# One core: modulation rows brought forward, and index scores computed between the slabs of two projection groups

## The reference, cut to what matters

```python
c_act = silu(c)
mod = c_act @ w_mod + b_mod                   # 6 x 2048: shift1, scale1, gate1, shift2, scale2, gate2
h = rms_norm(x, g_pre_mix) * (1 + scale1) + shift1
q, k, v, q_idx, k_idx, w_idx, pool_in, lru_in, lru_gate = split(h @ w_in)
dots = einsum('qhd,sd->qhs', q_idx, k_idx)    # 16 index heads of 64
score = einsum('qh,qhs->qs', w_idx, relu(dots)) / 32, then top 128 keys per query
logits = q k / sqrt(128) + rel_bias[bucket(distance)]
```

## Time and profile before

| | us |
|---|---|
| median of 3 runs | 2516.28 (2509.43 to 2518.47) |
| the profiled execution, its own time | 2509.14 |
| span of its instructions | 2507.0 |
| PE busy in the span | 2388.7 (95%) |
| DVE / ACT / POOL busy | 1213.4 / 684.5 / 362.5 |

### The profile page before, as it was taken

How to read it: one execution, slowest core, us unless ns; L and a number is a source line. 1 busy time by engine, 2 the same in 40 slices (tenths; PEclk the granted TensorE clock), 3 DMA queues, 4 the chain that set the end, 5 groups by cost and what they waited for, 6 DMA issues and landing times.

```text
span 2507.0 us, 27318 instructions
## 1 busy us (share of the span) xinstructions
PE 2388.7 (95%) x10722; PEld 1880.6 (75%) x10722; DVE 1213.4 (48%) x1586; ACT 684.5 (27%) x896; POOL 362.5 (14%) x247
## 2 busy tenths in 40 slices
PE   4898899999997999899999999999999999999997
PEld 1456687778776788788888888888888888888885
DVE  5536966699329765643333234343243332333336
ACT  2332624222326422422122122121121221221222
POOL 3543054444427200000000000000000000000000
PEclk8999999989999999999999999999999999999998
DMA  4987266733314276522332332323322333323324
GB/s 180 364 338 272 93 235 235 262 128 95 91 61 129 97 268 244 135 84 93 93 93 94 97 94 92 92 84 100 99 93 92 84 100 95 97 93 92 93 93 168
DMA packets 137504, 340.89 MB, mean 136 GB/s; under 512 B 15824, under 2 KB 17488, under 8 KB 123216
## 3 DMA queue, kind: packets, MB, share of 16 engines
q1 hardware_dynamic: 132208, 331.12, 39.6%
q10 hardware_dynamic: 5216, 8.66, 0.9%
HBM read 322.70 MB, written 16.79 MB: 135 GB/s over the span
## 4 chain that ended last, share of the span: by engine, by line
PE 85%; DVE 7%; DMA 3%; ACT 2%; issue 2%; ACTq 1%; POOL 0%; SPq 0%; DVEq 0%; POOLq 0%
PE psum L694 27%; PE psum L696 27%; PE psum L695 27%; DMA mod_slab<-in_w_mod 2%; DVE acc_a L1394 2%; DMA raw<-in_w_in 1%; PE psum L773 1%; PE psum L758 1%; PE psum L742 1%; PE psum L803 1%; ACT sq_out L1044 0%; DVE pt_lo L1712 0%; PE psum L735 0%; DVE probs L1699 0%; ACTq L1063 0%
## 5 line engine op out<-in xcount | busy, mean ns | idle before, releaser
L1755 DVE TENSOR_TENSOR w_lo<-raw,w_hi 128x1024 fp32r<-128x1024 f32 x256 | 311.7, 1224 | 744.1 <-ACT w_hi L1281 743.7
L694 PE MATMUL psum<-h_hi,w_hi 128*128 128x512 f32 (+1 forms) x1616 | 645.9, 400 | 11.5 <-POOL w_lo L634 5.5
L695 PE MATMUL psum<-h_lo,w_hi 128*128 128x512 f32 (+1 forms) x1616 | 644.6, 399 | 0.0
L696 PE MATMUL psum<-h_hi,w_lo 128*128 128x512 f32 (+1 forms) x1616 | 643.9, 398 | 0.0
L1281 ACT ACTIVATE w_hi<-raw 128x1024 fp32r<-128x1024 f32 x256 | 271.2, 1060 | 1014.9 <-PE psum L696 1005.8
L694 PE MATMUL psum<-w_hi,u_hi 128*128 128x512 f32 x1024 | 408.3, 399 | 0.0
L696 PE MATMUL psum<-w_hi,u_lo 128*128 128x512 f32 x1024 | 403.6, 394 | 0.0
L695 PE MATMUL psum<-w_lo,u_hi 128*128 128x512 f32 x1024 | 401.5, 392 | 0.0
L694 PEld LDWEIGHTS psum<-h_hi,w_hi 128*128 128x128 f32 (+1 forms) x1616 | 306.1, 189 | 91.3 <-issue 9.2
L696 PEld LDWEIGHTS psum<-h_hi,w_lo 128*128 128x128 f32 (+1 forms) x1616 | 306.1, 189 | 75.7 <-issue 0.2
L695 PEld LDWEIGHTS psum<-h_lo,w_hi 128*128 128x128 f32 (+1 forms) x1616 | 306.0, 189 | 74.3 <-issue 0.2
(11 more groups left out here) (256 smaller groups left out, 2064.1 us busy)
## 6 DMA issues: line engine op xcount, KB each, us to landing
raw<-in_w_mlp_up SPq DMA_DIRECT2D x128, 512.0 KB, 3.7
raw<-in_w_mlp_down SPq DMA_DIRECT2D x128, 512.0 KB, 3.7
mod_slab<-in_w_mod SPq DMA_DIRECT2D x48, 1024.0 KB, 5.9
raw<-in_w_in SPq DMA_DIRECT2D x88, 512.0 KB, 5.9
mod_ring<-in_w_mod_first SPq DMA_DIRECT2D x32, 1024.0 KB, 9.0
raw<-in_w_out SPq DMA_DIRECT2D x32, 512.0 KB, 5.8
slab<-in_w_mod SPq DMA_DIRECT2D x16, 1024.0 KB, 4.9
bias_s<-bias_out ACTq DMA_DIRECT2D x32, 256.0 KB, 6.1
```

Source lines behind the costliest of these rows:

```text
L694: nc.tensor.matmul(o, a_hi, b_hi, start=first, stop=False)
L695: nc.tensor.matmul(o, a_hi, b_lo, start=False, stop=False)
L696: return nc.tensor.matmul(o, a_lo, b_hi, start=False, stop=last)
L1755: V.tensor_tensor(w_lo[:, local % RING, :, :], raw[:, local % RING, :, :], w_hi[:, local % RING, :, :].bitcast(F32), ALU.subtract).then_in ...
```

## The change

At the start: the bias table and its shifted copy come inside the packed columns, so that ACT's eight DMAs are gone. The sums of squares use 32 columns of the ones matrix for each of four tiles side by side, in one bank; ACT copies that bank to `x_rows`, and one matmul with a selecting matrix `pick` adds the four rows and spreads them over all partitions. ACT squares a quarter of x at a time and stores one bias bank after each. `x_norm` follows the steps of the eighth bank, scales nothing, and two tiles of x are scaled in each block; `softplus` follows the third block. The memsets on POOL are put in another order, those of `stat` and `inv_n` after the table.

In the middle: the `dots` stages are gone. After each slab of g2 and g3 PE does the dots of two pairs (three after slabs 24 and 25, none after slab 31), in banks 4 to 7 in turn; the turn of the index weights follows slab 16. In ACT's loop the slab 19 + j is rounded and then the ReLUs of the pairs after slab 16 + j are taken. In DVE's loop the modulation slabs of slab 16 + j are added and then the dots of those pairs. The modulation slabs go three to two weight slabs up to slab 31, then one each up to slab 55. The two copies of the index key are issued by ACT, before it takes the high part of s1, and no longer by SP.

```diff
 MOD_EARLY = 2 * KD
 MOD_BLOCKS = KD // KS
 MOD_PROJ = 3 * KD
-MOD_DOTS = 3 * SG
-MOD_AGAIN = 3 * SG + 3
+MOD_AGAIN = 4 * SG
+MOD_MORE = 3 * SG
 def mods_beside(s):
-    if 2 * SG <= s < 3 * SG:
+    if 2 * SG <= s < 4 * SG:
         i = s - 2 * SG
         first = MOD_EARLY + 3 * (i // 2) + 2 * (i % 2)
         return [first] if i % 2 else [first, first + 1]
-    if MOD_AGAIN <= s < MOD_AGAIN + 2 * KD:
-        return [MOD_EARLY + KD + s - MOD_AGAIN]
+    if MOD_AGAIN <= s < MOD_AGAIN + MOD_MORE:
+        return [MOD_EARLY + MOD_MORE + s - MOD_AGAIN]
     return []
...
 STAGES = (
-    [("s0", "AD"), ("s1", "AD"), ("g2", "AD"), ("widx", "D")]
...
+DOT_PAIRS = TT * IH // 2
+PAIRS_AFTER = (2,) * SG + (3, 3) + (2,) * (SG - 3) + (0,)
+assert sum(PAIRS_AFTER) == DOT_PAIRS and sum(PAIRS_AFTER[:SG]) == DOT_PAIRS // 2
+DOT_BANK = 4
 def dots_of(n):
-    pair, n = divmod(n, 2 * IH)
-    return 2 * pair + n % 2, n // 2
+    return n % TT, n // TT
+def pairs_after(i):
+    return range(sum(PAIRS_AFTER[:i]), sum(PAIRS_AFTER[:i + 1]))
...
                 for g in mods_beside(s):
                     load_mod(g)
                 load_slab(s + 2)
-                if s == 2 * SG + 2:
-                    sp.wait_ge(idx_ready, 1)
-                    sp.dma_start(ki_hi[1][ID:P, :].bitcast(F32), ki_hi[0][0:ID, :].bitcast(F32)).then_inc(key_copied, 16)
-                    sp.dma_start(ki_lo[1][ID:P, :].bitcast(F32), ki_lo[0][0:ID, :].bitcast(F32)).then_inc(key_copied, 16)
-                if s == MOD_DOTS:
-                    for t in range(TT):
-                        load_mod(DOTS_MOD + t)
                 if s == MOD_AGAIN + 1:
                     sp.wait_ge(score_done, 1)
...
+            ch.link(nc.gpsimd.memset(pick[:], 0.0))
+            for q in range(4):
+                ch.put(nc.gpsimd.memset(pick[32 * q:32 * q + 1, :], 1.0))
             ch.wait()
             pool.sem_inc(consts, 1)
...
-            for k in range(KD):
-                pe.wait_ge(xsq_ready, k + 1)
-                last = nc.tensor.matmul(psum[:, XSUM_BANK, :], ones[:], x_sq[:, k, :], start=k == 0, stop=k == KD - 1)
+            pe.wait_ge(blk_ready, 1)
+            for q in range(TT):
+                bias_bank(q)
+                pe.wait_ge(xsq_ready, 4 * q + 4)
+                for j in range(4):
+                    last = nc.tensor.matmul(psum[32 * j:32 * j + 32, XSUM_BANK, :], ones[:, 0:32], x_sq[:, 4 * q + j, :],
+                                            start=q == 0, stop=q == TT - 1)
             last.then_inc(xsum_done, 1)
-            pe.wait_ge(blk_ready, 1)
-            for i in range(BIAS_FIRST):
+            pe.wait_ge(consts, 1)
+            pe.wait_ge(xrows_ready, 1)
+            nc.tensor.matmul(psum[:, XALL_BANK, :], pick[:], x_rows[:], start=True, stop=True).then_inc(xall_done, 1)
+            for i in range(TT, BIAS_FIRST):
                 bias_bank(i)
...
-            group(G_QI + 1, STAGE["g2"], features_out, h)
-            n = STAGE["widx"]
-            begin(n)
-            pe.wait_ge(widx_copied, 1)
-            for t in range(TT):
-                last = nc.tensor.transpose(bank(n, 0)[:, IH * t:IH * t + IH], widx_t[ID:KW, P * t:P * t + P],
-                                           ident[ID:KW, ID:KW])
-            last.then_inc(stage_done, 1)
-            pe.wait_ge(key_copied, 32)
-            for m in range(TT * IH // 4):
-                if m == 0:
+            def key_weights():
+                n = STAGE["widx"]
+                begin(n)
+                pe.wait_ge(widx_copied, 1)
+                for t in range(TT):
+                    last = nc.tensor.transpose(bank(n, 2)[:, IH * t:IH * t + IH], widx_t[ID:KW, P * t:P * t + P],
+                                               ident[ID:KW, ID:KW])
+                last.then_inc(stage_done, 1)
+            def dots_pair(n):
+                if n == 0:
+                    pe.wait_ge(key_copied, 32)
                     pe.wait_ge(idx_ready, 1 + IH // 4)
-                elif dots_of(4 * m)[1] == IH // 2:
+                elif n == 1:
+                    pe.wait_ge(widx_read, 1)
+                elif n >= 2:
+                    pe.wait_ge(relu_ready, 2 * n - 2)
+                if n == DOT_PAIRS // 2:
                     pe.wait_ge(idx_ready, 1 + IH // 2)
-                n = STAGE[f"dots{m}"]
-                begin(n)
-                for b in range(4):
-                    t, hd = dots_of(4 * m + b)
+                for k in (2 * n, 2 * n + 1):
+                    t, hd = dots_of(k)
                     tok = slice(P * t, P * t + P)
-                    last = three(bank(n, b), qi_hi[:, hd // 2, tok], qi_lo[:, hd // 2, tok], ki_hi[hd % 2][:],
+                    last = three(psum[:, dot_bank(k), :], qi_hi[:, hd // 2, tok], qi_lo[:, hd // 2, tok], ki_hi[hd % 2][:],
                                  ki_lo[hd % 2][:], True, True)
-                last.then_inc(stage_done, 1)
-            group(G_LRU, STAGE["g3"], features_out, h)
+                last.then_inc(dots_done, 1)
+            def after_g2(j):
+                if j == 0:
+                    key_weights()
+                for n in pairs_after(j):
+                    dots_pair(n)
+            def after_g3(j):
+                for n in pairs_after(SG + j):
+                    dots_pair(n)
+            group(G_QI + 1, STAGE["g2"], features_out, h, after=after_g2)
+            group(G_LRU, STAGE["g3"], features_out, h, after=after_g3)
...
-            act.wait_ge(consts, 1)
-            for q in range(4):
-                act.dma_start(rb[32 * q:32 * q + NBUCKET, :], rel_bias).then_inc(rb_in, 16)
-                act.dma_start(rb_prev[32 * q + 1:32 * q + NBUCKET, :], rel_bias[0:NBUCKET - 1, :]).then_inc(rb_in, 16)
             act.wait_ge(cols_in, 16)
             nc.scalar.activation(c_tmp[:], cols("c"), ACT.Tanh, scale=0.5).then_inc(c_tanh, 1)
             act.wait_ge(vec_ready, 1)
             nc.scalar.activation(lam_t[:, 1, :], lam_t[:, 0, :], ACT.Exp, scale=-1.0).then_inc(c_tanh, 1)
-            act.wait_ge(consts, 2)
-            for k in range(KD):
-                act.wait_ge(x_landed[k // 4], 16)
-                nc.scalar.activation(x_sq[:, k, :], x_t[:, k, :], ACT.Square).then_inc(xsq_ready, 1)
-            act.wait_ge(xsum_done, 1)
-            nc.scalar.activation(x_root[:], psum[:, XSUM_BANK, :], ACT.Sqrt, bias=eps_c[:], scale=1.0 / D).then_inc(root_ready, 1)
             def bias_store(i):
...
-            for i in range(BIAS_FIRST):
+            for q in range(TT):
+                act.wait_ge(x_landed[q], 16)
+                for k in range(4 * q, 4 * q + 4):
+                    nc.scalar.activation(x_sq[:, k, :], x_t[:, k, :], ACT.Square).then_inc(xsq_ready, 1)
+                bias_store(q)
+            act.wait_ge(xsum_done, 1)
+            nc.scalar.activation(x_rows[:], psum[:, XSUM_BANK, :], ACT.Copy).then_inc(xrows_ready, 1)
+            act.wait_ge(consts, 1)
+            act.wait_ge(xall_done, 1)
+            nc.scalar.activation(x_root[:], psum[:, XALL_BANK, :], ACT.Sqrt, bias=eps_c[:], scale=1.0 / D).then_inc(root_ready, 1)
+            for i in range(TT, BIAS_FIRST):
                 bias_store(i)
             split(0)
             split(1)
...
+                act.wait_ge(xn_ready, KS * b + KS)
                 h_high(0, 2 * b, x_t[:, 2 * b, :], h_hi)
...
-            for g in (1, 2):
-                s = split_to(s, SG * (g + 1) + 3)
+            def relus(pairs):
+                for n in pairs:
+                    act.wait_ge(dots_done, n + 1)
+                    for k in (2 * n, 2 * n + 1):
+                        if k >= 2:
+                            act.wait_ge(relu_used, k - 1)
+                        nc.scalar.activation(relu[:, k % 2, :], psum[:, dot_bank(k), :], ACT.Relu).then_inc(relu_ready, 1)
+            def index_high(g):
                 done("s1" if g == 1 else "g2")
                 for b in range(4):
                     o = psum[:, QI_BANK + b, :] if g == 1 else bank(STAGE["g2"], b)
                     nc.scalar.activation(qi_hi[:, 4 * (g - 1) + b, :], o, ACT.Copy).then_inc(act_hi, 1)
                 act.wait_ge(act_hi, 1 + 4 * g)
                 act.sem_inc(act_freed, 1)
-            for m in range(TT * IH // 4):
-                done(f"dots{m}")
-                for b in range(4):
-                    k = 4 * m + b
-                    if k >= 2:
-                        act.wait_ge(relu_used, k - 1)
-                    nc.scalar.activation(relu[:, k % 2, :], bank(STAGE[f"dots{m}"], b), ACT.Relu).then_inc(relu_ready, 1)
-                act.wait_ge(relu_ready, 4 * m + 4)
-                act.sem_inc(act_freed, 1)
+            act.wait_ge(idx_ready, 1)
+            for part in (ki_hi, ki_lo):
+                act.dma_start(part[1][ID:P, :].bitcast(F32), part[0][0:ID, :].bitcast(F32)).then_inc(key_copied, 16)
+            index_high(1)
+            for j in range(2 * SG):
+                s = split_to(s, 2 * SG + 4 + j)
+                if j == SG - 1:
```

(102 more changed lines are left out.)

21 lines of the change are left out of this document (10 added, 11 removed), and 1 row of the table STAGES.

## The result

The changed kernel takes 2564.70 us (median of 4 runs, 2558.27 to 2568.82), beside 2517.38 for the kernel before (median of 4): a ratio of 1.0189, 95% interval 1.0154 to 1.0223. The forecast was 2553 in 2510 to 2583, slower. The profiled execution has a span of 2556.3 us, 49.3 more than before.

What follows compares the result with a forecast made beforehand. PE carried 85% of the chain of waits; the change would make the middle a closed loop of waits. Start -26.5, middle +65, behind +3 gave +41.5 on 2509.14, 2550.6, taken as 2553; range 2510 to 2583.

Steps and rivals of the forecast that it cites:

- The loop: In g2 and g3, each round's additions, modulation slab, transfer, rounding and ReLU wait on one another: 14.0 us a round.
- Rival (a): In g2 and g3, PE stays the bound because three ready slabs cover the waits: 138 us, total 2472; chance 0.13.
- break-even round of 11.0 us: In the middle, the round length put as the point between gain and loss for the whole change.
- the signs named: Start row at 30 to 35 us; middle additions 13 to 15 us apart, PE 60 to 65% busy, DMA near 40 to 50%.
- The start: Up to the first modulation row: row at 33 us instead of 61.5, gain kept, net -26.5 us.
- The middle: From g2's first matmul to g3's end: g3 ends at 413.4 instead of 348.22, costing +65 us.
- Behind: After g3: PE may wait for weight slabs at g4's end, +3 us (0 to 8).
- Rival (b): In the middle, the loop holds but its transfer is quick: round 11.1 us, total 2512, no change; chance 0.08.
- The round: In the middle: rounding 1.06, ReLU and additions 3.6, modulation slab 2.58, transfer 6.7; 14.0 us with semaphores, bounds 13.2 and 16.
- The first round: At g2's start: first modulation slab ends at 201.2, then 6.7 + 1.06 + 3.6, so round 0 ends at 212.6.
- The rule: For the middle's 1 MB and 0.5 MB transfers: fixed 2.0 us plus bytes over 436 GB/s, 5.6 us; total near 2538.

Runs made afterwards that it cites:

- experiments 2 and 3: Changed kernel, with ACT taking ReLUs before rounding: 2471.75 us; or, for slabs 16 to 31, SP loading the weight slab before the step's modulation slabs: 2471.09 us.
- experiment 4: Changed kernel, but in steps 16 to 31 SP, after the same wait, issues the weight slab before the last modulation slab: 2529.01 us.
- start_only: The start of the changed kernel with the middle of the kernel before: 2488.44 us, ratio 0.9912 to the kernel before.
- middle_only: The middle of the changed kernel with the start of the kernel before: 2588.68 us, ratio 1.0304 to the kernel before.
- experiment 5: Changed kernel, but POOL starts its subtraction for slab 19 + j only when DVE's additions of round j are done: 2542.35 us, ratio 1.0116 to the kernel before.

## Why the prediction was right, step by step

**Which way, and through what.** The sign, the place and the mechanism were right. The loop was read from SP's and ACT's order before; its members are the rows of one round, and each cut of it (experiments 2 and 3) frees some 90 us. Rival (a), PE as the bound, fell as the changed kernel, and came true once the loop was cut: 137.9 us from g2 to g3's end, where it had 138, and 2471.75 for the whole, where it had 2472. The break-even round of 11.0 us fits: at 12.2 us a round (experiment 4) the kernel is 0.6% slower than before. Of the signs named, the bursts of additions came as said (14.5 to 14.9 us apart, but for one round of 16.8, the two with six additions and the turn from g2 to g3); the first modulation row at 37.55 missed the 30 to 35 without reaching 40, PE is busy for 71% of the middle and not 60 to 65, and the DMA engines stand at 38%, just under 40.

**The sum.** Between the two profiled executions the change costs 49.3 us where the terms made 41.5: the start gave 3.1 less, the middle cost 12 more, and what follows was 7.3 lower than forecast. So part of the nearness of 2553 to 2564.70 is luck, since the last term offset some of the others. Rival (b) is added up wrongly: 1.06 + 3.6 + 2.35 + 3.7 is a round of 10.7 us, 10.8 with semaphores, and gives about 2508, not 11.1 and 2512; it is no change either way.

**The round: 14.64 us instead of 14.0.** Its terms against the measured ones: rounding and the first ReLU 1.06 + 0.60, measured 1.58 from the rounding's start to the first addition (214.51 to 216.09); the additions 3.0, measured 4.5 (201.45 to 205.96); the modulation slab 2.58, measured 2.35; from its end to the rounding 6.7, measured 6.2 (208.31 to 214.51) and 6.0 in the round before. So the transfer was shorter than I took it and the additions longer, because the price of an addition came from a stretch in which POOL was idle, while in the new order POOL's subtraction starts with them. That term was mis-sized by 1.5 us a round, some 21 us in all, and partly made up by the transfer. The hint stood in the earlier trace rows: a modulation slab of 3.22 us from 205.60, with POOL's subtraction in the same trace from 204.27 to 206.67. One round has a transfer of 8.3 us (344.3 to 352.6), near the long end of the forecast; the other 13 have 6.0 to 6.5.

**The first round.** Forecast to end 212.6 - 193.0 = 19.6 us after g2's start, measured 191.48 - 169.60 = 21.9: the first modulation slab is done 9.6 us after it, not 8.2. With rounds of 14.64 and that, the middle is 77 and not 65.

**The start: 23.4 instead of 26.5.** The first row stands at 37.55, not 33. Bank 0 was done at 15.4, not 14; the third copy waited 2.16 us for a store; ACT's fourth store stood in front of the copy of the sums; and the selecting matmul took 2.05 us at the lower clock, not 1.0. The claim that what is gained there lasts was right: `start_only` keeps it to the end. Softplus cost 1.5 us in block 3 (82.45 to 98.98 instead of the usual 15.05), where I had 2.

**Behind: -4.3 instead of +3.** The wait at the end of g4 did not come. The 4.3 us themselves are within the scatter of single executions: for the same work behind g3 `middle_only` takes 2586.1 - 424.2 = 2161.9 us, the kernel with the ReLUs first 2160.0 and the one with the slab first 2155.4, beside 2154.5 in the changed kernel and 2158.8 before. The waits scatter with it: the kernel before loses 1.7 and 3.8 us to two waits of PE for `w_lo`, the changed kernel has neither but 2.3 us before the gates (L886), and `middle_only` has one of 1.8 us for `w_lo` and 2.2 before the gates.

**The rule.** For the pair of transfers the changed kernel has 6.0 to 6.5 us in 13 of 14 rounds. The estimate after the Trainium skill (DMA: Bandwidth & Descriptors, Anatomy of one DMA), made for another issuing path, is 5.6 us. It is about as far below most of the measured rounds as my 6.7 is above them. With the 0.5 MB first (experiment 4) ACT had it 3.8 us after the addition. An estimate by the same formula of the Trainium skill is 3.2 us for that one.

## What to carry to other kernels

When work of several engines is interleaved, write the wait graph of one round before anything else: what each engine does ahead of the step for which the next one waits, back to the first. If the path closes on itself within a round, its sum and not the busiest engine is the period, and a transfer that is issued just behind the last member costs its whole latency every round. The cure is one line of order on any member: let the result out first and prepare the next input behind it, or issue the load one round earlier; and price an engine's instruction in the company it will have, not in the stretch where it ran alone.

## What the runs showed of the hardware

DVE's `scalar_tensor_tensor` and POOL's `tensor_tensor`, both on operands in SBUF, took turns in these traces: whichever began first kept its time, and the other was stretched by about as much. In the changed kernel the first addition of the round takes 2.46 us instead of 0.75, from 201.45 to 203.91: POOL's subtraction of 2.35 us, begun 0.44 us earlier, is over at 203.36. The next three take their 0.75. The row is that of the groups of instructions between 201.3 and 203.2 us:

```profile
L1620 DVE SCALAR_TENSOR_TENSOR score<-relu,w_idx,score 128x512 f32<-128x512 f32 x1 | 2.5, 2459 | 7.6 <-ACT relu L1160 7.6
```

With the two held apart (experiment 5) all 64 additions took 743 to 755 ns. There DVE's modulation slab began 0.16 us ahead of POOL: it kept its 2.35 us, POOL's subtraction took 4.43 instead of 2.36, and DVE's second slab 4.40.

Waits of PE can cost twice. Behind most of its longer waits in the middle TensorE was granted 1.2 GHz for a while. After an idle time of 3.88 us a dot's matmuls started 0.43 us apart, at a granted clock of 0.50 from 202.0 to 204.8:

```profile
201.96 0.79 PE L704 MATMUL psum<-ki_hi,qi_hi 128*128 128x512 f32 x1 [3.88 <-ACT relu L1160]
202.55 0.63 PE L705 MATMUL psum<-ki_lo,qi_hi 128*128 128x512 f32 x1
202.97 0.63 PE L706 MATMUL psum<-ki_hi,qi_lo 128*128 128x512 f32 x1
```

At 2.4 GHz they start 0.23 apart, and they did so behind the waits of 1.54 and 1.67 us in the first round (187.44 and 190.76) and behind one of 2.71 us (305.71). The mean over the middle was 0.83 in the changed kernel, 0.94 in experiment 4, where most waits of PE are 1.4 to 1.7 us, and 0.99 with the loop cut. It did not set the round here: PE was idle for some 4.5 us of each (232 - 164 us over 15 rounds), and behind the slow matmuls of this round it still waited 4.06 us for ACT's next ReLU (216.59).
